# A decoder layer of gated MLP, convolution, cross-attention and routed experts on one core: ones matmuls in waits, gate values on VectorE, another order at the end of the prompt attention, sample values turned by transposes

## What is computed

```
z = rms_norm(x) @ w_in                      # u | v | a | b, 512 columns each
u = gelu(z_u);  v = layer_norm(gelu(z_v))   # gates: per head of 128 channels, times ln_g plus ln_b
a_out = u * (tril(W_s) @ v + b_s)           # per chunk of 128 tokens
b_out = silu(layer_norm(conv31(a * sigmoid(b))))
x = x + [a_out | b_out] @ w_out
x = x + softmax(q k^T / 16) v @ w_o         # 256 memory tokens, 4 heads; samples have their own caches
x = x + sum over 2 chosen of 32 experts (one group of 4, two of its 8): w2(silu(w1 x) * w3 x)
y = rms_norm(x)
```

## Time and profile before

| | |
|---|---|
| median of 3 runs | 679.25 (678.85 to 681.24) |
| profiled execution | 680.17 |
| its span | 678.4 |
| mean granted TensorE clock | 0.944 of full |
| busy: TensorE, its weight loads, VectorE, ScalarE, GpSimd | 594.8, 466.9, 317.4, 197.9, 79.8 |
| moved by DMA | 181.57 MB |

### The profile page before, as it was taken

The page is one execution under the profiler, slowest core; times in us unless marked ns, Lnnn a source line. Parts: engine busy times, 40 slices in busy tenths (PEclk is TensorE's granted clock), DMA queues, the critical chain, the costliest instruction groups (busy, mean ns, idle before and its releaser), DMA issues.

```text
span 678.4 us, 11951 instructions
## 1 busy us (share of the span) xinstructions
PE 594.8 (88%) x4899; PEld 466.9 (69%) x4899; DVE 317.4 (47%) x625; ACT 197.9 (29%) x337; POOL 79.8 (12%) x131
## 2 busy tenths in 40 slices
PE   5999999899999999999999957999999987589810
PEld 5999996577899999984889844546646654246400
DVE  4678787789644374778422273211111111011147
ACT  6422323145734344445022231111111111011032
POOL 0000000700002200000212201112112111010100
PEclk9999999999999999999989975999999999689965
DMA  8863110326554314779599495999999999999663
GB/s 325 306 243 124 63 64 3 127 84 212 164 167 149 125 64 137 271 243 424 208 391 393 160 399 199 402 421 418 420 417 420 421 418 421 420 421 414 250 271 127
DMA packets 35652, 181.57 MB, mean 268 GB/s; under 512 B 8943, under 2 KB 10127, under 8 KB 16765
## 3 DMA queue, kind: packets, MB, share of 16 engines
q1 hardware_dynamic: 26733, 165.62, 62.1%
q0 software_dynamic: 5600, 12.76, 5.0%
q10 hardware_dynamic: 3264, 2.42, 1.1%
HBM read 174.94 MB, written 15.61 MB: 281 GB/s over the span
## 4 chain that ended last, share of the span: by engine, by line
PE 65%; SPq 14%; DMA 8%; DVE 8%; issue 3%; ACT 1%; DVEq 0%; POOLq 0%; ACTq 0%
PE ps L1714 13%; PE ps L1716 13%; PE ps L1715 13%; SPq L628 9%; PE ps L2146 7%; SPq L637 4%; PE ps L2174 4%; DMA w<-exp_w 4%; PE ps L1821 4%; PE ps L1710 3%; DMA raw<-caches 2%; PE ps L1923 2%; DVE ttr_out L1354 1%; PE ps L1987 1%; DVE x L1662 1%
## 5 line engine op out<-in xcount | busy, mean ns | idle before, releaser
L1714 PE MATMUL ps<-xH,w_h 128*128 128x260 f32 x480 | 138.7, 289 | 0.4 <-DVE xL L1368 0.2
L1716 PE MATMUL ps<-xL,w_h 128*128 128x260 f32 x480 | 136.3, 284 | 0.0
L1715 PE MATMUL ps<-xH,w_l 128*128 128x260 f32 x480 | 136.1, 284 | 0.0
L2146 PE MATMUL ps<-w,xeT 128*64 128x256 f32 (+2 forms) x1024 | 121.5, 407 | 12.5 <-DMA w<-exp_w 10.3
L2146 PEld LDWEIGHTS ps<-w,xeT 128*64 128x64 f32 (+2 forms) x1024 | 82.9, 145 | 56.2 <-issue 29.5
L1714 PEld LDWEIGHTS ps<-xH,w_h 128*128 128x128 f32 x480 | 91.1, 190 | 5.0 <-issue 4.3
L1715 PEld LDWEIGHTS ps<-xH,w_l 128*128 128x128 f32 x480 | 91.1, 190 | 0.1
L1716 PEld LDWEIGHTS ps<-xL,w_h 128*128 128x128 f32 x480 | 91.1, 190 | 0.0
L1059 DVE TENSOR_TENSOR w_l<-raw,w_h 128x2048 fp32r<-128x2048 f32 x27 | 61.8, 2289 | 27.8 <-ACT w_h L741 27.6
L2174 PE MATMUL ps<-w,aT 128*64 128x512 f32 (+2 forms) x256 | 60.3, 628 | 15.8 <-DVE aT L1627 12.0
L741 ACT ACTIVATE w_h<-raw 128x2048 fp32r<-128x2048 f32 x27 | 51.6, 1911 | 22.2 <-PE ps L1716 19.3
(11 more groups left out here) (352 smaller groups left out, 857.0 us busy)
## 6 DMA issues: line engine op xcount, KB each, us to landing
w<-exp_w SPq DMA_DIRECT2D x96, 1024.0 KB, 24.0
raw<-weights SPq DMA_DIRECT2D x27, 1024.0 KB, 5.3
raw<-caches SPq DMA_DIRECT2D x16, 1024.0 KB, 7.4
qb<-q_rows POOLq DMA_DIRECT2D x4, 1024.0 KB, 6.7
yr<-y_rows SPq DMA_DIRECT2D x4, 1024.0 KB, 7.9
xT<-x_turned SPq DMA_DIRECT2D x4, 520.0 KB, 7.4
raw<-x_prompt SPq DMA_DIRECT2D x4, 512.0 KB, 12.0
x_rows<-x ACTq DMA_DIRECT2D x4, 512.0 KB
```

What stands on the lines that cost most here:

```text
L1714: pe.matmul(out, h1, h2, start=start, stop=False)
L1715: pe.matmul(out, l1, h2, start=False, stop=False)
L1716: return pe.matmul(out, h1, l2, start=False, stop=stop)
L2146: last = pe.matmul((mm[0][half, j, 0:FF], ta[1][half, 0:FF])[h], xeT[j][:, k, half], w13[s][:, h, k, :], start=k == 0, stop=k == KT_D - 1)
```

## The change

1. `kept_busy(out, count)`: TensorE multiplies a 128x128 tile of ones by itself into a PSUM bank that nobody reads. 14 such at the start, 4 before the counts of the routing and 2 behind them, 20 before the list of slots, 12 before the first gathered rows and 4 after them.
2. `V_TAPS` from 9 to 11: two taps of 31 go from TensorE to VectorE, and `PART_AT` says where.
3. Gate values wholly on VectorE, 40 instructions in place of 20, and GpSimd's 10 go. The mean of the memory's squares moves ahead of them, its reciprocal behind the first tile.
4. The end of the prompt attention in another order on VectorE and ScalarE.
5. Sample values: `so` becomes `so0` and `so1`, each of four transposes; of the last half unit of `wo` ahead of them (steps 4 to 7 of unit (3, 0)) two steps stay ahead, and two go behind the first logits. The copies out take the 8 rows from whole 128x128 blocks.

```diff
-V_TAPS = 9
+V_TAPS = 11
...
@@ scalar
             exps(3)
+            values_out(0)
+            norms(3)
             split_h(25)
-            norms(3)
-            values_out(0)
             values_out(1)
...
-            act.wait_ge(tv_ready, TV_AT["so"] + 1)
-            act.activation(xH[:, :, SEQ:T], tv[TV_AT["so"] % 2][:, 0:8 * NS].rearrange("p (k s) -> p k s", k=8),
-                           ACT.Copy).then_inc(oh_ready, 1)
+            for b in range(2):
+                act.wait_ge(tv_ready, TV_AT[f"so{b}"] + 1)
+                ins = act.activation(of_samples(xH, b), own_rows(tv[TV_AT[f"so{b}"] % 2]), ACT.Copy)
+            ins.then_inc(oh_ready, 1)
...
@@ vector
-            PART_AT = {4: 3, 5: 4, 6: 4, 7: 3, 8: 2, 9: 3, 10: 3, 11: 3, 14: 3}
+            PART_AT = {4: 3, 5: 4, 6: 4, 7: 3, 8: 2, 9: 3, 10: 3, 11: 3, 12: 2, 13: 2, 14: 3, 15: 2}
...
-            for j, (t0, n_t) in enumerate(TILES):
+            for j in range(NT):
                 for h in range(HEADS):
-                    last = dve.tensor_scalar(row, row, mv[0:n_t, j, h, 0:1], mv[0:n_t, j, h, 1:2], ALU.subtract, ALU.mult)
+                    row, n_t, c = v_row(j, h)
+                    last = dve.scalar_tensor_tensor(row, row, mv[0:n_t, j, h, 0:1], ln_g[0:n_t, c], ALU.subtract, ALU.mult)
                 last.then_inc(v_norm, 1)
+                dve.wait_ge(v_norm, j + 1)
+                for h in range(HEADS):
+                    row, n_t, c = v_row(j, h)
+                    last = dve.scalar_tensor_tensor(row, row, mv[0:n_t, j, h, 1:2], ln_b[0:n_t, c], ALU.mult, ALU.add)
+                last.then_inc(v_ready, 1)
...
             score_max(3)
-            sample_scores(5)
+            sample_scores(5, range(2))
             score_sums(3)
+            sample_scores(5, range(2, 4))
+            values_low(0)
+            sample_scores(6, range(2))
+            values_low(1)
             split_l(25)
-            values_low(0)
-            values_low(1)
-            sample_scores(6)
             values_low(2)
+            sample_scores(6, range(2, 4))
             values_low(3)
             sample_scores(7)
...
@@ tensor
+            def kept_busy(out, count):
+
+                for _ in range(count):
+                    pe.matmul(out, ones[:], ones[:], start=True, stop=True)
+
+            pe.wait_ge(dve_made, 1)
+            kept_busy(ta[0][:, 0:P], 14)
             first_pair()
...
-            half_of_wo(3, 0, range(4, 8))
+            half_of_wo(3, 0, range(4, 6))
...
-            pe.wait_ge(tv_used, TV_AT["or1"] + 1)
-            out = open_tv("so")[:, 0:8 * NS].rearrange("p (k s) -> p k s", k=8)
-            one_row = ident[:].rearrange("p (j g m) -> p g j m", g=2, m=BAND // 2)[:, :, :, 0]
-            for k in range(8):
-                last = pe.matmul(out[:, k, :], o_s[:, k * P:(k + 1) * P], one_row, start=True, stop=True)
-            last.then_inc(tv_ready, 1)
+            for b in range(2):
+                pe.wait_ge(tv_used, TV_AT[f"or{b}"] + 1)
+                out = open_tv(f"so{b}")
+                for k in range(4):
+                    last = turn(out[:, k * P:(k + 1) * P], o_s[:, (4 * b + k) * P:(4 * b + k + 1) * P])
+                last.then_inc(tv_ready, 1)
             for k in EARLY:
                 half_of_logits(k, 0)
-            pe.wait_ge(tv_used, TV_AT["so"] + 1)
+            half_of_wo(3, 0, range(6, 8))
+            pe.wait_ge(tv_used, TV_AT["so1"] + 1)
...
+            pe.wait_ge(mm_used, len(MM_ORDER))
+            kept_busy(mm[1][:, 1, 0:P], 4)
             pe.wait_ge(who_ready, 1)
-            pe.wait_ge(mm_used, len(MM_ORDER))
...
+            kept_busy(mm[1][:, 1, 0:P], 2)
             pe.wait_ge(route_by_dve, ROUTE_BY_DVE["less"])
...
+            pe.wait_ge(ta_used, len(TA_ORDER))
+            kept_busy(ta[1][:, 0:P], 20)
             in_bands(open_tv("list"), hot_no, hot_ready)
...
+            kept_busy(ta[1][:, 0:P], 12)
             pe.wait_ge(tv_used, len(TV_ORDER))
-            pe.wait_ge(ta_used, len(TA_ORDER))
             gathered_columns(0, 0, 1)
+            kept_busy(ta[1][:, 0:P], 4)
...
@@ gpsimd
-            for j, (_, n) in enumerate(TILES):
-                row = v_tok[:, j, :] if j < 4 else v_s[0:n]
-                pool.wait_ge(v_norm, j + 1)
-                pool.tensor_tensor(row, row, ln_g[0:n], ALU.mult).then_inc(v_scaled, 1)
-                pool.wait_ge(v_scaled, j + 1)
-                pool.tensor_tensor(row, row, ln_b[0:n], ALU.add).then_inc(v_ready, 1)
```

More of the change, by code:

```diff
@@ L139 @@
             + ["lm0", "lm1", "lv0", "lv1", "kt0", "kt1", "kt2", "kt3"] + ["rs2", "rs3"]
-            + ["ss", "sp", "or0", "or1", "so", "con", "r2", "lg", "pos", "list", "ids", "rs_list", "rs_ids"])
+            + ["ss", "sp", "or0", "or1", "so0", "so1", "con", "r2", "lg", "pos", "list", "ids", "rs_list", "rs_ids"])
 TV_AT = {key: v for v, key in enumerate(TV_ORDER)}
@@ L498, in trunk_kernel, with own_rows, of_samples @@
         route_done = sem("route_done")
+        def own_rows(x):
+            return x.rearrange("p (k j g m) -> p k g j m", j=4, g=2, m=BAND // 2)[:, :, :, :, 0]
+        def of_samples(x, b):
+            return x[:, 4 * b:4 * b + 4, SEQ:T].rearrange("p k (g j) -> p k g j", g=2)
         def mm_of(m):
@@ L649, in _ @@
             sp.wait_ge(l_ready, W_AT[("wo", 3)] + 1)
-            sp.wait_ge(tv_ready, TV_AT["so"] + 1)
+            sp.wait_ge(tv_ready, TV_AT["so1"] + 1)
             load_gate_up(2, 2)
@@ L1218, in _, with v_row @@
                 part_taps(2 if i < 3 else len(part_todo))
+            dve.wait_ge(mem_sq, 2)
+            dve.tensor_scalar(m_ss[:], m_ss[:], 1.0 / D, EPS, ALU.mult, ALU.add).then_inc(m_mean, 1)
             dve.wait_ge(v_root, 1)
             link(dve.reciprocal(mv[:, :, :, 1], mv[:, :, :, 1]))
-            for j, (t0, n_t) in enumerate(TILES):
+            def v_row(j, h):
+                n_t = TILES[j][1]
+                return (v_tok[:, j, :] if j < 4 else v_s[0:n_t])[:, h * P:(h + 1) * P], n_t, slice(h * P, (h + 1) * P)
+            for j in range(NT):
                 for h in range(HEADS):
-                    row = (v_tok[:, j, :] if j < 4 else v_s[0:n_t])[:, h * P:(h + 1) * P]
-                    last = dve.tensor_scalar(row, row, mv[0:n_t, j, h, 0:1], mv[0:n_t, j, h, 1:2], ALU.subtract, ALU.mult)
+                    row, n_t, c = v_row(j, h)
+                    last = dve.scalar_tensor_tensor(row, row, mv[0:n_t, j, h, 0:1], ln_g[0:n_t, c], ALU.subtract, ALU.mult)
                 last.then_inc(v_norm, 1)
[L1228 to L1231, removed]
+                dve.wait_ge(v_norm, j + 1)
[3 more added lines that the diff above has]
+                last.then_inc(v_ready, 1)
+                if j == 0:
+                    dve.wait_ge(m_root, 1)
+                    dve.reciprocal(m_ss[:], m_ss[:]).then_inc(m_mean, 1)
             def keys_in(h):
@@ L1432, in _ @@
                 dve.tensor_copy(o_s[:, 512 * b:512 * b + 512], src).then_inc(tv_used, 1)
+            for b in range(2):
+                src = own_rows(take(f"so{b}"))
+                dve.wait_ge(oh_ready, 5)
+                dve.tensor_tensor(of_samples(xL, b), src, of_samples(xH, b).bitcast(F32), ALU.subtract).then_inc(tv_used, 1)
             residual(3, 0)
-            src = take("so")[:, 0:8 * NS].rearrange("p (k s) -> p k s", k=8)
-            dve.wait_ge(oh_ready, 5)
-            dve.tensor_tensor(xL[:, :, SEQ:T], src, xH[:, :, SEQ:T].bitcast(F32), ALU.subtract).then_inc(tv_used, 1)
             src = take("con")
```

1 line of the change is left out of this document (removed).

## The result

| | before | changed |
|---|---|---|
| median of 5 runs | 679.25 (678.54 to 681.24) | 675.06 (674.37 to 675.30) |
| ratio of medians, 95% interval | | 0.9939 (0.9923 to 0.9955) |
| span of the profiled execution | 678.4 | 673.3 |
| mean granted clock | 0.944 | 0.956 |
| busy: TensorE, VectorE, GpSimd | 594.8, 317.4, 79.8 | 601.7, 320.0, 67.2 |

The kernel is 4.2 us faster, 0.6%. The forecast was a gain of 6.6 and a time of 672.7, with a range of 668.5 to 676.5.

A forecast was written before the change was run, and what follows sets the result against it. TensorE was taken to bound the kernel up to about 384 us, and DMA of expert weights from 430 to 620. Terms -0.3 -2.2 +2.0 -1.0 -1.4 -3.7 sum to -6.6, giving median 672.7, range 668.5 to 676.5.

The forecast's parts named there:

- start: Kernel start: ones matmuls bring the full clock, third step 0.6 earlier, but token norms wait for `diag`; gain 0.3.
- taps: Convolution: two fewer taps on TensorE at 1.09 each, VectorE's added work hidden; -2.2.
- gate values, and on to `values`: VectorE's forty instructions take 10 to 13 and end before TensorE turns `v_s`; hidden, worth nothing.
- attention: End of prompt attention: VectorE waits 4.3 for head 3's queries ahead of block 6, delaying `values(3)`; cost +2.0.
- samples: Turning the samples' values with eight full transposes instead of 8-column matmuls; -1.0.
- clock in `wo`, and to the counts: After the samples' values: dense columns keep the clock from falling at 342.3; -1.4.
- routing and first round: Ones matmuls hold full clock through routing and round 0, the weight stream's hole closes; -3.7, at least -1.3.
- 13.4 without a wait: End of prompt attention: VectorE's remaining work after the queries land, so scores end at 326.95 instead of 324.95.
- The first rival: Routing: the clock falls anyway despite the dense ones matmuls; -4.2 in sum, 675.0; chance 0.17.
- The second: Prompt attention: the new order gains TensorE's 1.07 wait if queries land earlier; -9.7 in sum, 669.5; chance 0.15.
- That ones might not raise the clock: Routing stays at 1.2 GHz and the ones matmuls delay it; +6.5, 685.8; chance of slower 0.04.
- The third rival: Samples' values: transposes do not hold the clock, so the 1.4 stays lost; -5.2 in sum, 674.1; chance 0.12.

The follow-up runs named there:

- b: Changed kernel without the ones matmuls of the routing, the 14 at the start kept; 677.60, ratio 0.9980.
- c: Changed kernel without the 14 ones matmuls at the start; 677.44, ratio 0.9975.
- d: Changed kernel with `V_TAPS` 9 and its old table, so 22 taps on TensorE; 678.70, ratio 1.0000.
- i: Changed kernel with gate values as before (20 instructions on VectorE, 10 on GpSimd) and the mean of the memory's squares behind them; 679.84, ratio 1.0011.
- j: Changed kernel with the samples' values turned as before: four steps of `wo`, eight matmuls of 8 columns, one split; 675.43, ratio 0.9941.
- a: Changed kernel with the end of the prompt attention in the old order on VectorE and ScalarE; 672.36, ratio 0.9900.
- f: Changed kernel with 3 more ones matmuls behind each of the two lists of slots; 673.13, ratio 0.9921.
- k: The kernel before, unchanged, run again for a second profile; 678.75.
- e: Changed kernel with `split_l(25)` and `values_low(1)` ahead of the first half of block 6's scores on VectorE; 670.70, ratio 0.9866.
- h: Changed kernel with the edits of e and f together; 670.63, ratio 0.9877.
- l: Kernel h with 14 ones matmuls instead of 20 ahead of the list; 669.99, ratio 0.9871.
- g: Changed kernel without the 12 ones matmuls ahead of the first gathered rows; 674.91, ratio 0.9940.

## Why the prediction was right, and where not

| term | forecast | profile |
|---|---|---|
| start | -0.3 | +0.3 |
| taps | -2.2 | -4.1 |
| gate values, and on to `values` | 0 | +0.5 |
| attention | +2.0 | +2.9 |
| samples | -1.0 | -0.6 |
| clock in `wo`, and to the counts | -1.4 | -1.4 |
| routing and first round | -3.7 | -2.6 |
| rest | 0 | -0.1 |
| sum | -6.6 | -5.1 |

The sign, and faster by over 0.5%, were right, and the sum was off by 1.5 in the profiles and by 2.4 in the medians. That it came this close is in part luck: two of the terms (taps, and the clock in `wo`) were won against things that the one profile of before had and its second did not have, or had shorter. Nor do the parts add up: put back one at a time, b, c, d, i and j lose 2.5, 2.4, 3.6, 4.8 and 0.4 in the medians and a wins 2.7, which is 11.0 together, where the whole change brought 4.2.

- *Start.* "The third step starts 0.6 earlier" (0.84) and "`diag`, whatever TensorE does" held; `diag` itself came 0.3 later, behind ScalarE, which waited for later loads. Over the profiles the norms lie between 24.0 and 25.6, those without the ones at 24.3 and 24.8, so no gain there is shown. What the 14 brought (2.4 in c) lies elsewhere, where the forecast did not look.
- *Taps.* Two are 2.4 here when the stop of 1.71 is taken off before (29.31), and 2.1 by d: as forecast. The rest of the 4.1 is that stop, which the forecast did not cost at all.
- *Gate values.* As a term, 0 was right, and so were the 10 to 13 for the forty (11.3), with the reason given against 28. The +0.5 behind them is also between the two profiles of before (170.3 and 170.8). "So it is hidden and worth nothing" was wrong for the part: it looked at `v_s` alone, and at the old end of the taps. Experiment i shows what else stood behind the gate values. By its trace the -2.2 of the taps is only to be had with the mean moved ahead.
- *Attention.* The mechanism, the place and the 4.3 of VectorE's wait were right (4.27). The step that failed is "13.4 without a wait": TensorE lost its clock in the 2.51, its last values took 5.33 instead of 3.60, and VectorE waited 1.48 for them. The earlier trace rows has a wait of 1.43 at this same place before, which the forecast did not carry over. With the clock held VectorE does not wait there, and the cost is 1.6 in b and 0.7 in f, below the 2.0; in the changed kernel it is 2.9, in d 5.4.
- *Samples.* 0.6 instead of 1.0. The eight transposes gave 0.8: the logits start 0.97 behind them, where 0.87 was forecast and the 8-column matmuls needed 1.79. The two steps behind the logits then took 0.92, where ahead of them they took 0.73.
- *Clock in `wo`.* "With dense columns there it should not fall: -1.4" is refuted as a cause. The time was won against the one profile of before, but j and k have the 8-column matmuls and a clock of 1.00.
- *Routing.* The failed step is "The 12 take 2.6 and end before the rows land": they took 5.47 and ended 2.5 after the first rows. Up to the gather the forecast of 2.45 held (2.8), and round 0 took the forecast time; between them 1.8 were lost. So the hole did not close, but moved. The first rival was half right: the clock did fall, only later. That its 675.0 is the measured time is chance: the routing gained 2.6, not its 1.3. The second, a gain from the order of the attention, is refuted for this order; e wins its 1.07 and a little more. That ones might not raise the clock is refuted: h's 20 began at half clock (0.50 from 392 to 394), ran 0.42 apart, and ran 0.22 apart at their end (0.89 from 397 to 399).

The third rival is not settled at its own place, as nothing fell there. Elsewhere TensorE in the changed kernel ran only transposes from 384.28 until the ones at 391.93, and the clock rose under them:

```profile
387.00:388.00 1.00, 1.00 (x6) 0.77 (x5) 0.86 (x5) 0.74 (x2) 0.00 (x0) 0.50 1.04 410
388.00:389.00 1.00, 1.00 (x8) 0.74 (x6) 0.89 (x4) 0.59 (x2) 0.00 (x0) 0.88 1.14 352
389.00:390.00 1.00, 0.65 (x6) 0.42 (x5) 0.84 (x5) 0.95 (x2) 0.00 (x0) 1.00 1.00 221
```

The rule that the forecast cited from the Trainium skill (TensorE: Matmul & The Clock Gate, section on PE-mode transpose) does not hold for the transposes of this kernel.

## What to carry to other kernels

When two engines wait for each other, ask of every instruction moved ahead what stands behind it on its own engine: with half a block of scores ahead of `values_low(1)` the new order cost 2.7, and with it behind (e) VectorE's order took 1.4 off the stage that the old one needs. A part whose own gain is nothing can be the condition of another: after shortening TensorE's path, look for the next work that was just in time, here the root of the memory's mean. And a dip of the clock in a single profile is no property of the code: take a second profile before a term rests on it.

## What the runs showed of the hardware

**The clock falls in one of several places.** In the same stretch of code the clock differs from kernel to kernel, and in before and k between two executions of one. From the counts to the gather the 20 ones (14 in l) gave either 11.9 to 12.0 (changed, a, d, e, f, i, l) or 14.8 to 14.9 (c, g, h, j), no faster than none (14.1 to 14.6). In the first seven the clock had fallen once ahead of the counts (changed: 0.66 from 384 to 389) and then held (1.00 from 389 to 405). In the other four it held there (h: 1.00 from 379 to 390) and fell at the small matmuls just ahead of the 20 (0.65 from 390 to 392). Ones keep a clock, but where it has just fallen the same 20 take 7.1 to 7.2 instead of 4.7 and delay what waits behind them. The Trainium skill (TensorE: Matmul & The Clock Gate, Part 1) says that the monitor runs freely, so that at its start the same kernel shows other counts of slow matmuls from run to run. k against before shows the like in the middle of a kernel, 1.00 against 0.72.

**A block of instructions that comes late.** In before, k and c TensorE stands in the taps for 1.71, 0.74 and 1.75 with no releaser. At that time two weight blocks of 1 MB fill the DMA queues, and a packet of the queue of instructions is among them: at 125.5 in before, 124.9 in k, 126.0 in c. The timeline of c and k, and the DMA queues of c from 125.5 to 126.0 (packets, MB, share):

```profile
128.35 0.63 PE L1847 MATMUL ps<-glu,dw 32*32 32x512 f32 x4 [1.75 <-issue]
```

```profile
127.27 2.77 PE L1821 MATMUL ps<-glu,dw 32*32 32x512 f32 x68 [0.74 <-issue]
```

```profile
q1 hardware_dynamic: 24, 0.20, 92.7%
q8 instruction: 1, 0.02, 11.6%
```

In the other eleven profiles such a packet comes between 121.0 and 123.3 (in e, whose taps began 2.6 later, at 124.5), and TensorE does not stop. It follows the packet before it by 7.1 to 8.1 in the three, and by 5.1 to 6.7 in the eleven; g has a further one at 126.0 without a stop, so the time alone does not decide. All three with the stop are those without the 14 ones at the start, and all eleven without it have them. That the ones shift which instructions a block holds, or when it is fetched, fits this, and would be most of the 2.4 that c lost. Whose instructions a packet holds the profile does not say, and no other padding was tried, so the cause stays open.
